# Rows of the first expert block built on TensorE by one-hot products, and a layer norm applied in halves

## The reference

```python
e_idx, gw = route(x2, router_w, router_bias)      # 2 experts of 16 for each token, sigmoid scores
...
dest = pad_start[sorted_e] + jnp.arange(A) - start[sorted_e]        # slot of each (token, expert) pair
slot_tok = jnp.full((P,), T).at[dest].set(sorted_tok)               # token of each slot
xp = jnp.concatenate([x2, zeros])[slot_tok]                         # rows of x, in slot order
def expert_block(args):                                             # 128 slots of one expert
    xb, e = args
    h = jax.nn.silu(xb @ w_gate[e]) * (xb @ w_up[e])
    return h @ w_down[e]
yp = lax.map(expert_block, (xp.reshape(n_blk, MOE_BLOCK, D), blk_e))
y = segment_sum(yp[dest] * gw, sorted_tok)
```

## Time and profile before

| what | value |
|---|---|
| median of 3 runs | 2500.0 us (2495.45 to 2500.74) |
| the profiled execution's own time | 2492.09 us |
| its span | 2490.4 us, 35127 instructions |
| TensorE (PE) busy | 2198.6 us (88%) |
| VectorE (DVE) busy | 1317.7 us (53%) |
| ScalarE (ACT) busy | 989.8 us (40%) |
| GpSimd (POOL) busy | 199.4 us (8%) |
| chain that ended last, by engine | PE 74%, DVE 14%, ACT 6%, issue 3%, DMA 2% |
| mean granted TensorE clock | 0.93 |

### The profile page before, as it was taken

How to read it: one execution, slowest core, us unless ns; L and a number is a source line. 1 busy time by engine, 2 the same in 40 slices (tenths; PEclk the granted TensorE clock), 3 DMA queues, 4 the chain that set the end, 5 groups by cost and what they waited for, 6 DMA issues and landing times.

```text
span 2490.4 us, 35127 instructions
## 1 busy us (share of the span) xinstructions
PE 2198.6 (88%) x13178; PEld 1861.2 (75%) x13178; DVE 1317.7 (53%) x2054; ACT 989.8 (40%) x1642; POOL 199.4 (8%) x241
## 2 busy tenths in 40 slices
PE   5799898998988779999698989899898887999993
PEld 5778875988878757777587887598887875777772
DVE  2476367452153556556767726845215445665567
ACT  2255466223231335455334536622324123554552
POOL 0000011000000222000200000100000022210004
PEclk9899998999998689999899999899999877999997
DMA  3531121122100469999611112023210036999995
GB/s 146 203 106 35 35 85 38 66 102 68 65 29 26 163 239 371 377 382 372 226 60 34 35 35 85 24 80 102 68 51 35 26 132 228 372 378 382 378 369 199
DMA packets 78244, 386.56 MB, mean 155 GB/s; under 512 B 10393, under 2 KB 11433, under 8 KB 43305
## 3 DMA queue, kind: packets, MB, share of 16 engines
q1 hardware_dynamic: 54608, 327.70, 35.1%
q0 software_dynamic: 10448, 31.44, 3.5%
q10 hardware_dynamic: 13064, 25.75, 2.8%
HBM read 338.78 MB, written 46.07 MB: 155 GB/s over the span
## 4 chain that ended last, share of the span: by engine, by line
PE 74%; DVE 14%; ACT 6%; issue 3%; DMA 2%; ACTq 0%; POOL 0%; DVEq 0%; POOLq 0%
PE bank L1923 35%; PE bank L2341 9%; PE bank L2315 8%; PE bank L2305 7%; PE bank L1939 2%; PE bank L2050 2%; PE bank L2221 2%; DVE weight_slots_parts L1292 2%; PE bank L2290 1%; PE bank L2040 1%; ACT weight_slots_parts L855 1%; PE bank L2069 1%; PE bank L2254 1%; ACT x_transposed L995 1%; PE bank L2180 1%
## 5 line engine op out<-in xcount | busy, mean ns | idle before, releaser
L1923 PE MATMUL bank<-weight_slots_parts,x_transposed_parts 128*128 128x256 f32 x2496 | 469.7, 290 | 14.2 <-ACT mixer_region L918 13.9
L1923 PEld LDWEIGHTS bank<-weight_slots_parts,x_transposed_parts 128*128 128x128 f32 x2496 | 401.6, 198 | 15.9 <-ACT mixer_region L918 15.1
L1729 DVE TENSOR_TENSOR weight_slots_parts<-weight_slots,mixer_region_parts 128x2048 fp32r<-128x2048 f32 x140 | 323.7, 2331 | 85.7 <-ACT mixer_region_parts L1129 85.5
L1292 DVE TENSOR_TENSOR weight_slots_parts<-weight_slots,weight_slots_parts 128x2048 fp32r<-128x2048 f32 x58 | 132.9, 2292 | 300.7 <-ACT weight_slots_parts L855 300.2
L1923 PE MATMUL bank<-x_transposed_parts,weight_slots_parts 128*128 128x256 f32 (+1 forms) x1024 | 267.0, 349 | 24.4 <-issue 13.2
L1129 ACT ACTIVATE mixer_region_parts<-weight_slots 128x2048 fp32r<-128x2048 f32 x140 | 261.0, 1909 | 20.5 <-ACT x_transposed L1196 18.2
L2341 PE MATMUL bank<-weight_slots,x_transposed 128*128 128x512 f32 x560 | 246.4, 593 | 0.0
L1923 PEld LDWEIGHTS bank<-x_transposed_parts,weight_slots_parts 128*128 128x128 f32 x1024 | 183.9, 197 | 48.5 <-issue 14.5
L2315 PE MATMUL bank<-mixer_region_parts,x_transposed_parts 128*128 128x256 f32 x1120 | 207.7, 283 | 1.2 <-DVE weight_slots_parts L1729 1.2
L2305 PE MATMUL bank<-mixer_region_parts,x_transposed_parts 128*128 128x512 f32 x560 | 196.0, 422 | 4.2 <-DVE x_transposed_parts L1734 4.2
L2341 PEld LDWEIGHTS bank<-weight_slots,x_transposed 128*128 128x128 f32 x560 | 103.4, 190 | 117.9 <-issue 101.7
(11 more groups left out here) (274 smaller groups left out, 3672.8 us busy)
## 6 DMA issues: line engine op xcount, KB each, us to landing
weight_slots<-in_w_gate SPq DMA_DIRECT2D x70, 1024.0 KB, 7.3
weight_slots<-in_w_up SPq DMA_DIRECT2D x70, 1024.0 KB, 7.0
weight_slots<-in_w_down SPq DMA_DIRECT2D x70, 1024.0 KB, 7.7
weight_slots<-in_w_in SPq DMA_DIRECT2D x20, 1024.0 KB, 5.1
slots_y<-x_transposed ACTq DMA_DIRECT2D x70, 256.0 KB, 7.2
weight_slots<-in_wkv_mem SPq DMA_DIRECT2D x16, 1024.0 KB, 4.9
slots_y<-mixed SPq DMA_DIRECT2D x2, 6912.0 KB, 33.3
weight_slots<-in_w_out SPq DMA_DIRECT2D x8, 1024.0 KB, 4.9
```

The costliest lines, as they stand in the source:

```text
L1292: v.tensor_tensor(half_lo(name), half_raw(name), half_hi(name).bitcast(F32), ALU.subtract).then_inc(w_lo, 1)
L1729: v.tensor_tensor(lo, raw, hi.bitcast(F32), ALU.subtract).then_inc(moe.low_ready, 1)
L1923: ins = pe.matmul(ps, lhs[i](k), rhs[j](k), start=k == 0 and a == 0, stop=k == ks - 1 and a == 2)
```

## The change

Block 0 no longer takes its rows by way of HBM. A new column block of the constants holds the numbers 0 to 127 (`slot_numbers`, loaded by SP in each layer ahead of the first expert's weights). `place` compares it with each chunk's lower slot number, which gives a 128 x 128 one-hot matrix `pick[c]` (token by slot) for each chunk. TensorE multiplies each with that chunk of x, float32 as it is, and sums over the chunks: 12 matmuls of 128x512 into banks 5 and 6 (`b0`), of which six stand before the last chunk's transposes in `ROUTER_ORDER`, four between its scores and its ranks, two at the end. ScalarE copies the two halves to `first_x`, and `turn_block(first_x)` takes the place of the first gather. The 12 scatters stay, since the later blocks need them. GpSimd's first token read is block 1's now, after `ids_ready`, and it gathers block 1 into `xb` without waiting for block 0's transposes. On TensorE and ScalarE the wait for `ids_ready` and the `value_load` of the number of blocks now come after the block's transposes and high part. VectorE makes the first block's low part ahead of `low_part(3, 4)`.

Beside that the last chunk's second norm is made in halves: the statistics of its left half are taken before its right half arrives, and the left half has a signal of its own, for which its first transposes wait. In `ln_apply` the wait for the inverse deviation stands between the two passes instead of ahead of both.

```diff
 ROUTER_ORDER = ([("wx", 4, 0), ("wx", 4, 1)] + [("x3", c, h) for c in range(4) for h in range(2)] + [("rl", 0), ("wx", 5, 0),
-                ("x3", 4, 0), ("x3", 4, 1), ("rl", 1), ("rk", 0), ("wx", 5, 1), ("rk", 1), ("x3", 5, 0), ("x3", 5, 1),
-                ("rl", 2), ("rk", 2)])
+                ("x3", 4, 0), ("x3", 4, 1), ("rl", 1), ("rk", 0), ("wx", 5, 1), ("rk", 1), ("b0", (0, 1, 2)), ("x3", 5, 0), ("x3", 5, 1),
+                ("rl", 2), ("b0", (3, 4)), ("rk", 2), ("b0", (5,))])
...
     for key in ROUTER_ORDER:
+        if key[0] == "b0":
+            if key[1][0] == 0:
+                add(("b0", 0), (5,))
+                add(("b0", 1), (6,))
+            continue
         add(key, {"wx": (5, 6, 7), "x3": (0, 1, 2), "rl": (4,), "rk": (3,)}[key[0]])
...
+        pick = [y_t[:, 2560 + c * P:2560 + c * P + P] for c in range(NC)]
+        first_x = y_t[:, 3584:4608]
+        slot_numbers = y_t[:, 3328:3456]
...
         x_scaled = sem("x_scaled")
+        numbers_loaded = sem("slot_numbers_loaded")
+        picks_ready = sem("first_block_picks_ready")
+        x_left_ready = sem("last_chunk_left_half_ready")
         scattered = sem("slots_scattered")
...
                     tile_filled(sp, ("wx", NC - 1, 0))
+                    sp.dma_start(slot_numbers, consts[:, C_PICK:C_ROWS]).then_inc(numbers_loaded, 16)
                     load_gate(0, 0, moe.ga_loaded)
...
                     pool.wait_ge(scattered, 192 * l + 16 * 2 * NC)
-                    nc.gpsimd.dma_start(block_tokens[:, :], by_block[0, :, :]).then_inc(moe.ids_loaded, 16)
-                    pool.wait_ge(x_saved, 96 * l + 16 * NC)
-                    pool.wait_ge(moe.ids_loaded, 16)
-                    gather_block()
-                    pool.wait_ge(moe.x_loaded, 16)
                     pool.wait_ge(ids_ready, 1 * l + 1)
...
                     load_tokens(slice(1, 2))
+                    pool.wait_ge(x_saved, 96 * l + 16 * NC)
                     def next_block(b, at):
-                        pool.wait_ge(moe.xT_filled, 2 * b + 2)
-                        pool.wait_ge(moe.ids_loaded, 16 * b + 32)
+                        pool.wait_ge(moe.ids_loaded, 16 * b + 16)
                         pool.sem_inc(moe.gather_turn, 1)
                         gather_block()
-                        pool.wait_ge(moe.x_loaded, 16 * b + 32)
+                        pool.wait_ge(moe.x_loaded, 16 * b + 16)
                         pool.sem_inc(moe.gather_turn, 1)
...
                     for c in range(NC):
+                        if c:
+                            pool.wait_ge(moe.xT_filled, 2 * c + 2)
                         next_block(c, slice(c + 2, c + 3))
+                        if c == 0:
+                            pool.wait_ge(moe.xT_filled, 2)
                         nc.gpsimd.tensor_scalar(x[:, c, :], x[:, c, :], ALPHA, None, ALU.mult).then_inc(x_scaled, 1)
                     with pool.Fori(NC, n_blocks - 1) as b:
+                        pool.wait_ge(moe.xT_filled, 2 * b + 2)
                         next_block(b, bass.ds(b + 2, 1))
...
                         now[0] = l
-                    act.wait_ge(ids_ready, 1 * l + 1)
-                    n_blocks = act.value_load(r_nbi[0:1, 0:1], min_val=NE, max_val=BLOCKS)
-                    act.sem_inc(moe.g_ready, 1)
-                    act.sem_inc(moe.yl_ready, 1)
-                    act.sem_inc(moe.y_stored, 32)
+                    for h in range(2):
+                        drain_copy(("b0", h), first_x[:, 512 * h:512 * h + 512], 512)
...
                     block_xT()
+                    act.wait_ge(ids_ready, 1 * l + 1)
+                    n_blocks = act.value_load(r_nbi[0:1, 0:1], min_val=NE, max_val=BLOCKS)
+                    act.sem_inc(moe.g_ready, 1)
+                    act.sem_inc(moe.yl_ready, 1)
+                    act.sem_inc(moe.y_stored, 32)
...
                         dve.wait_ge(ln_rows_loaded[i // NC], 32 * l + 32)
-                        dve.wait_ge(ln_rstd, 18 * l + i + 1)
                         step(v.scalar_tensor_tensor(out=x[:, c, :], in0=x[:, c, :], scalar=st[:, o:o + 1], in1=lng,
                                                     op0=ALU.subtract, op1=ALU.mult))
+                        dve.wait_ge(ln_rstd, 18 * l + i + 1)
                         v.scalar_tensor_tensor(out=x[:, c, :], in0=x[:, c, :], scalar=st[:, o + 1:o + 2], in1=lnb,
...
                         step(v.tensor_scalar(sa, sa, FAR, None, ALU.add))
+                        dve.wait_ge(numbers_loaded, 16 * l + 16)
+                        for c in range(c0, c0 + n):
+                            v.tensor_scalar(pick[c], slot_numbers, r_slots[:, c:c + 1], None,
+                                            ALU.is_equal).then_inc(picks_ready, 1)
                         v.tensor_copy(slot_ids[:, c0:c0 + n], sa).then_inc(slots_ready, 1)
...
                     low_part(0, 1)
+                    stats = st[:, 70:82]
+                    v.bn_stats(stats[:, 0:6], x[:, 5, 0:512])
                     residual_half(5, "wx", 1)
...
                     tile_drained(dve, ("wx", 5, 1))
-                    ln_stats(NC + 5, 5)
-                    ln_apply(NC + 5, 5)
+                    step(v.bn_stats(stats[:, 6:12], x[:, 5, 512:D]))
+                    v.bn_aggr(st[:, 42:44], stats).then_inc(ln_var, 1)
+                    own(ln_var)
+                    for h in range(2):
+                        xh, w = x[:, 5, 512 * h:512 * h + 512], slice(512 * h, 512 * h + 512)
+                        step(v.scalar_tensor_tensor(out=xh, in0=xh, scalar=st[:, 42:43], in1=lng[:, w], op0=ALU.subtract, op1=ALU.mult))
+                        if h == 0:
+                            dve.wait_ge(ln_rstd, 18 * l + NC + 6)
+                        v.scalar_tensor_tensor(out=xh, in0=xh, scalar=st[:, 43:44], in1=lnb[:, w], op0=ALU.mult,
+                                               op1=ALU.add).then_inc((x_left_ready, x_ready)[h], 1)
+                    own(x_left_ready)
+                    own(x_ready)
                     place(1)
...
+                    low_block_xT(0)
                     low_part(3, 4)
-                    low_block_xT(0)
...
                             _, c, h = key
-                            pe.wait_ge(x_ready, 12 * l + NC + c + 1)
+                            if key == ("x3", 5, 0):
+                                pe.wait_ge(x_left_ready, l + 1)
+                            else:
+                                pe.wait_ge(x_ready, 12 * l + NC + c + 1)
                             turn4(key, lambda k: x[:, c, (4 * h + k) * P:(4 * h + k + 1) * P])
+                        elif key[0] == "b0":
+                            if key[1][0] == 0:
+                                first_ps = take(("b0", 0)), take(("b0", 1))
+                            for c in key[1]:
+                                pe.wait_ge(picks_ready, 6 * l + c + 1)
+                                for h in range(2):
+                                    ins = pe.matmul(first_ps[h][:, :], pick[c], x[:, c, 512 * h:512 * h + 512],
+                                                    start=c == 0, stop=c == NC - 1)
+                                    if c == NC - 1:
+                                        done(ins, ("b0", h))
                         elif key[0] == "rl":
...
+                    for bk in range(8):
+                        if bk not in (5, 6):
+                            pe.wait_ge(drained[bk], USES_BEFORE_EXPERTS[l][bk])
+                    def turn_block(source):
+                        for h in range(2):
+                            if source is first_x:
+                                tile_drained(pe, ("b0", h))
+                            for k in range(4):
+                                q = 4 * h + k
+                                ins = pe.transpose(banks[h][:, k * P:(k + 1) * P], source[:, q * P:(q + 1) * P], ident)
+                            ins.then_inc(moe.xT_filled, 1)
+                    turn_block(first_x)
                     pe.wait_ge(ids_ready, 1 * l + 1)
...
                     pe.sem_inc(moe.y_filled, 1)
-                    for bk in range(8):
-                        pe.wait_ge(drained[bk], USES_BEFORE_EXPERTS[l][bk])
-                    def turn_block():
-                        for h in range(2):
-                            for k in range(4):
-                                q = 4 * h + k
-                                ins = pe.transpose(banks[h][:, k * P:(k + 1) * P], xb[:, q * P:(q + 1) * P], ident)
-                            ins.then_inc(moe.xT_filled, 1)
                     parts = [expert_part(i) for i in range(6)]
-                    pe.wait_ge(moe.x_loaded, 16)
-                    turn_block()
...
                         if not last:
-                            pe.wait_ge(moe.x_loaded, 16 * b + 32)
-                            turn_block()
+                            pe.wait_ge(moe.x_loaded, 16 * b + 16)
+                            turn_block(xb)
```

8 lines of the change are left out of this document (5 added, 3 removed).

## The result

The changed kernel took 2459.11 us (median of 4 runs, 2455.27 to 2475.81) against 2500.37 (4 runs): ratio 0.9851, 95% interval 0.9804 to 0.9898. Six more runs on a chip shared with experiments gave 0.9863 (0.9835 to 0.989). It is faster, as forecast, but by 34 to 37 us by these ratios and by 32.6 in the profiled executions (2459.43 against 2492.09), where the forecast had 20. The ratios are those of the mean times; the two medians lie 41.3 us apart. The forecast for the median was 2480.0 and its range began at 2472.

What follows compares the result with a forecast made beforehand. Bound by TensorE's 27.4 us wait per layer for block 0's gathered x; 1.0 + 8.5 + 0.75 us in layer 1 and 1.0 + 8.0 + 0.75 in layer 2 make 20.0, for a median of 2480.0 us, range 2472 to 2489.

Steps and rivals of the forecast that it cites:

- Removed, and the six and four products: Scatter, token read and gather leave the path; six products fill idle time before the last transposes, four take 5.5 us.
- R 1.0 us earlier: R is the end of the router's ranks, forecast at 869.9 instead of 870.89 in layer 1.
- all warm: Bound for the end of the ranks with everything at the upper clock: 868.8, 2.1 us earlier.
- S = R + 9.5: S, the start of block 0's gate product, comes 9.5 us behind the ranks' end, shrinking that by 8.5 and 8.0 us.
- the path it named second: If all is warm, VectorE's table and low part end last before block 0's gate product, 9.0 us behind the ranks.
- The cold path: Last two products and transposes cold, then ScalarE's high part and value_load: gate product about 9.85 us behind the ranks.
- Hidden behind S: VectorE's 10.4 us of work after the gate product's start hidden by 0.5; block 1's x has 5 us to spare.
- The moved wait, 0.75 us a layer: Only one norm, in the cross-attention, is in the chain: 0.75 us a layer; the others lie under products.
- The clock stays up: Rival: granted clock up from the products on, 13.3 and 12.8 us in the two layers, 2474 us; chance 0.17.
- Cold products: Rival: products run cold from the start, ranks end 7.6 us later, 2498 us; chance 0.07.
- exposed weight loads: Rival: float32 weight loads don't hide under cold products, 4.6 us a layer more, 2507 us; chance 0.03.
- a start not passed on: Rival: late x for block 1 or late VectorE after block 0's start loses half the gain, 2490 us; chance 0.08.

Runs made afterwards that it cites:

- e2: Kernel before with only the wait for the inverse deviation moved between the two passes of ln_apply: 2479.62 us, 0.9931 of the kernel before.
- e12: Kernel before with only the moved wait in ln_apply, measured again on another chip session: 2475.12 us, 0.9934 of the kernel before.
- e3: Kernel before with the moved wait and the last chunk's norm in halves, no products: 2482.78 us, 0.995 of the kernel before.
- e1: The whole change once more, unaltered, against the kernel before: 2464.61 us, 0.9863.
- e8: The whole change with the last chunk's norm in one piece instead of halves: 2462.51 us, 0.9877 of the kernel before.
- e7: The whole change with the block count signalled by itself and block 0's low part ahead of the table's end: 2462.41 us, 0.9865 of the kernel before.
- e4: The whole change with the ln_apply wait back ahead of both passes (halves keep their moved wait): 2474.93 us, 0.9924 of the kernel before.
- e11: The whole change plus twelve repeated 128x256 products ahead of cross_half(4, 0) in layer 2 alone: 2459.12 us, 0.9852 of the kernel before.
- e10: Kernel before plus seven repeated 128x256 products ahead of cross_half(4, 0) in each layer, nothing removed: 2488.26 us, 0.997 of the kernel before.
- e5: Kernel before with the wait moved only in the six norms behind the mixer: 2491.12 us, 0.9988 of the kernel before.
- e9: Kernel before with the wait moved only in the cross-attention's norms: 2493.97 us, 0.9989 of the kernel before.

## Why the forecast was wrong, by its steps

*Removed, and the six and four products: right.* Warm and back to back, six took 5.40 us (0.90 each, forecast 0.86), the transposes behind them 1.04 (1.03), and the last chunk's 5.41 us of idle time was filled. The four took 5.38 (5.5), at a granted clock of 0.68.

*R 1.0 us earlier: too small, by the clock of the ranks.* D shrank by 2.2 and 1.8 us by the table and by 1.8 in both layers by the ranks' own end, near the forecast's "all warm" bound of 2.1. The mask came 1.0 us earlier (15.3 us behind the last residual instead of 16.3; forecast 1.1), but the ranks, which the forecast left at 1.9 us, took 1.07. They do in all twelve layers that have the four products ahead of them, and take 1.89 in the sixteen that don't. The moved wait alone brings the mask 0.6 us forward (e2, e12), the halves without products another 1.1 (e3: 14.6); the products take 0.7 of that back and give 0.8 at the ranks, which is why halves and products don't add (e1, e8).

*S = R + 9.5: right within 0.9, by the path it named second.* E is 9.1 and 8.9 us (8.8 and 8.6 from the ranks' own end), where the VectorE path was put at R + 9.0 and ScalarE's at R + 9.85; the steps of the latter as written add up to 9.4. The two products behind R ran warm (1.98 us), so the table was last; the chain shows it in both layers of the change, and e7 by taking 1.0 us more off in layer 1. `is_equal` cost 0.29 us against 0.25. The cold path exists too: in layer 1 of e4 and e11 and in layer 2 of e8 the granted clock was 0.50 during these two products and the transposes, and E was 10.1 us. In e4 the same two products took

```profile
871.55 3.78 PE L2291 MATMUL bank<-x,mixed 128*128 128x512 f32 x4 [1.81 <-DVE mixed L1744]
```

and the chain goes from them through the transposes and ScalarE's high part to VectorE's low part.

*Hidden behind S: right.* VectorE, in order of time:

```profile
875.60 2.42 DVE L1309 TENSOR_TENSOR mixer_region_parts<-mixer_region,mixer_region_parts 128x2176 fp32r<-128x2176 f32 x1 [0.96 <-DVE mixed L1840]
878.76 0.42 DVE L1852 TENSOR_TENSOR x_transposed<-x_transposed,bank 128x256 f32<-128x256 f32 x1 [0.73 <-PE bank L2365]
```

It was free 10.1 us behind S and wanted 10.9 behind it, with 0.7 us to spare. Block 1's gather was issued at 871.17 and landed at 875.26, and its transposes followed at 881.65 unwaited:

```profile
871.17 1.01 POOL L751 DMA_INDIRECT x_transposed<-x_rows,block_tokens  x1 [2.16 <-issue]
```

F was 0.7 and 1.8 us longer than before in the profile of the change and 1.8 and 3.1 in e1, but 1.2 and 0.9 shorter in layer 1 of e8 and e7 and 0.4 longer in layer 2; among the kernels without products it lies between 326.1 and 329.4 in layer 1 and between 382.6 and 383.7 in layer 2, where the change and e1 exceed that and e7, e8 and e11 don't. So a loss of a microsecond or two behind S can't be told from the spread; one small wait for a low part is in layer 2, at 2069.76, 0.35 us.

*The moved wait, 0.75 us a layer: this is the step that failed*, in the words "The others lie under products." They don't. The chain of before runs through all six norms behind the mixer; they and those of the cross-attention take 3.7 to 3.8 us off A and 2.3 off B in each layer of e12, and still 2.4 and 0.8 in layer 2 of e2, where less of it arrives. The row that the forecast rested on the earlier trace rows was one of many: it priced one norm near the router and none at the other places that the edited function `ln_apply` is called from. Measured alone, the moved wait gave 17 and 16 us (e2, e12) where the sum had 1.5.

*A second part of the same step.* C is not of one length: it goes with where the granted clock first falls in it. Six kernels with the wait moved have 51.5 us in layer 2; before has 47.9 twice, the first profile of the whole change 44.8 twice. C depends on the granted clock and not on the work (e10: 3.0 us less in both layers, nothing removed, the first fall 0.1 to 0.2 us sooner behind the start of C). That the moved start of C is what moves the fall within it fits this, but two executions of one kernel (e2 and e12) differ as much in layer 2, so it isn't shown. So the moved wait gives A to D 9.7 to 10.3 us in a layer where C falls to 44.8 and 0.3 in one where it rises to 51.5 (e12 and e2, the same kernel). The forecast had no term for it.

*The sum as it was.* From the two profiles: forecast 20.0; E 1.3 more, R 2.0 more; A 7.7 and B 4.6 where the norms had 1.5, thus 10.8 more; C 6.2; F 2.6 less. That is 37.7, of which this execution lost 5.9 in the stretch between the layers' experts and norms, and gained 0.6 ahead of the first norms and 0.2 behind the last: 32.6, the difference of the two spans. The ratios' 34 and 37 us lie near the 37.7, in part by chance: in e1's profile, the same kernel, A to F give 25.2, since C of layer 2 was 51.5 there and F longer.

*The rivals.* "The clock stays up" was half right: up until 852 and from 857.4, but the gate product of block 0 took 7.96 us all the same, so its 1.5 us a layer at S did not come; of what it foresaw, the warm ranks did. Cold products, exposed weight loads and a start not passed on did not happen. The Trainium skill, TensorE: Matmul & The Clock Gate, "What's actually happening", calls the throttled state the default that activity lifts; the trace agrees as far as the 1.00 in the filled stretch goes, and the 0.68 stands behind narrow scores.

*What stays open.* Which clock C gets in a given execution: there is one profile for each kernel, and e1 and the first profile of the whole change, the same kernel, differ in layer 2 by 6.8 us in C and 9.6 in A to D. How often each case comes was not measured; and that e5 and e9 give 3 us each (on two chips) and e2 and e12 17 and 16 is explained by C only as far as the single profiles go (A to D gain 3.9 and 0.3 in e5, 6.0 and -2.5 in e9, 10.3 and 0.3 in e2, 10.2 and 9.7 in e12). No run here tells what in the chip fixes the moments at which the clock changes.

## What to carry to other kernels

Before an edit in a helper is priced, list every place that calls it and look whether the chain of before passes there; one row from near the main change is no sample. A wait of 0.7 us that repeats in a run of short steps on the chain costs its whole sum (3.6 us over six norms here), and is cheap to cover by the first pass that doesn't need the value.

A stretch in which the granted clock falls and rises, as C with its narrow scores and ranks between wide products, has no fixed length: here the same work took 44.8, 47.9 or 51.5 us, with the first fall of the clock within 1.6 us of the same place. So such a stretch belongs in the range of a forecast, and an edit is judged by cuts at the same instructions over several executions, not by its total alone.

Products that replace a gather pay by where they stand: ten of twelve in idle time are nearly free, all twelve behind the last dependence cost nearly what the gather did.

## What was not expected of the chip

- The same 284 to 288 matmul records, with 3.6 us of idle time (3.9 in one layer), took 44.4 to 51.5 us; the mean granted clock was 0.81 to 0.70.
- Fourteen added products made the kernel before 7.5 us faster (4.7 to 10.2); in its profile C is 3.0 us shorter in each layer and B, which holds them, 0.7 and 0.8 longer.
- The first wide products behind 10.6 us of back-to-back 128x16 scores ran at half clock, for 3.0 to 4.3 us, though TensorE had not been idle during the scores; in layer 1 of before the granted clock was 0.51 from 822.00 to 828.20, during them, and 0.51 from there to 832.50.
- The same eight rank records took 1.07 us in all twelve layers with four wide products ahead of them and 1.89 in the sixteen without.
- Six runs of one kernel on one chip: 2451.3 us at a mean clock of 0.948, 2470.9 at 0.937.
